# A decoder layer on one NeuronCore: order of transposes and units at the FFN entry, and the waits of the down steps

## What is computed

```python
x = x + rms_norm(mix @ w_o[l], attn_post_g[l])
h = rms_norm(x, ffn_pre_g[l])
y = conv_glu_ffn(h, w_gate[l], w_up[l], conv_w[l], conv_b[l], w_down[l])
x = x + rms_norm(y, ffn_post_g[l])

def conv_glu_ffn(h, w_gate, w_up, conv_w, conv_b, w_down):
    g = h @ w_gate                       # (256, 8192)
    u = h @ w_up
    ...                                  # g = causal conv over 3 tokens + conv_b
    return (gelu(g) * u) @ w_down
```

## Time and profile before

| | us |
|---|---|
| Time, median of 3 runs (1455.94 to 1456.43) | 1456.36 |
| The profiled execution | 1457.93 |
| Its span in the trace | 1454.9 |
| TensorE products busy | 1442.3 (99%) |
| VectorE busy | 1096.9 (75%) |
| ScalarE busy | 690.4 (47%) |
| GpSimd busy | 131.2 (9%) |

### The profile page before, as it was taken

One profiled execution on the slowest core, in us unless ns is written; L12 is line 12 of the kernel. 1 busy time (PEld: TensorE's weight loads), 2 busy tenths in 40 slices (PEclk: granted clock), 3 DMA queues, 4 the chain that ended last, 5 costly groups with the idle time before them and its releaser, 6 DMA issues.

```text
span 1454.9 us, 20961 instructions
## 1 busy us (share of the span) xinstructions
PE 1442.3 (99%) x6786; PEld 1208.1 (83%) x6786; DVE 1096.9 (75%) x1725; ACT 690.4 (47%) x855; POOL 131.2 (9%) x128
## 2 busy tenths in 40 slices
PE   9999999999999999999999999999999999999997
PEld 9888888888878888888888888888888888888886
DVE  6768686965688998888998888998888555555455
ACT  6445444554465444444444444444454444444443
POOL 0716160710000000000000000000000000000000
PEclk9999999999999999999999999999999999999999
DMA  7755565555566666666666666666665656666653
GB/s 257 221 185 164 175 199 174 170 164 181 167 209 197 191 195 191 189 200 189 195 194 189 191 197 190 199 189 192 193 192 178 206 192 191 196 190 193 195 189 128
DMA packets 141459, 276.24 MB, mean 190 GB/s; under 512 B 9040, under 2 KB 39024, under 8 KB 141168
## 3 DMA queue, kind: packets, MB, share of 16 engines
q1 hardware_dynamic: 140608, 274.71, 62.6%
q10 hardware_dynamic: 816, 1.09, 0.2%
HBM read 273.67 MB, written 2.10 MB: 190 GB/s over the span
## 4 chain that ended last, share of the span: by engine, by line
PE 96%; DVE 2%; DMA 1%; issue 1%; ACT 0%; DVEq 0%; ACTq 0%; POOL 0%; POOLq 0%
PE psum L1585 22%; PE psum L1381 20%; PE psum L1385 20%; PE psum L1383 20%; PE psum L1348 7%; PE psum L1352 4%; DMA stage<-in_w_qkv 1%; PE psum L1426 0%; DVE up_T L1117 0%; PE psum L1266 0%; PE psum L1432 0%; DVE y_out L1252 0%; DVE w_lo L802 0%; PE psum L1366 0%; PE psum L1425 0%
## 5 line engine op out<-in xcount | busy, mean ns | idle before, releaser
L466 ACT CAST w_hi<-stage 128x1024 fp32r<-128x1024 f32 x509 | 535.1, 1052 | 724.1 <-PE psum L1385 453.5
L802 DVE TENSOR_TENSOR w_lo<-stage,w_hi 128x1024 fp32r<-128x1024 f32 x509 | 633.4, 1245 | 309.9 <-ACT w_hi L466 298.6
L1381 PE MATMUL psum<-w_hi,hT 128*128 128x512 f32 x1144 | 446.4, 390 | 0.0
L1385 PE MATMUL psum<-w_hi,hT 128*128 128x512 f32 x1144 | 445.2, 389 | 0.0
L1383 PE MATMUL psum<-w_lo,hT 128*128 128x512 f32 x1144 | 445.1, 389 | 0.0
L1585 PE MATMUL psum<-w_hi,hT 128*128 128x512 f32 x1024 | 275.4, 389 | 0.7 <-DVE w_lo L802 0.7
L1385 PEld LDWEIGHTS psum<-w_hi,hT 128*128 128x128 f32 x1144 | 214.7, 188 | 44.8
L1381 PEld LDWEIGHTS psum<-w_hi,hT 128*128 128x128 f32 x1144 | 214.7, 188 | 44.5 <-DVE hT L831 0.3
L1383 PEld LDWEIGHTS psum<-w_lo,hT 128*128 128x128 f32 x1144 | 214.8, 188 | 44.2
L1585 PEld LDWEIGHTS psum<-w_hi,hT 128*128 128x128 f32 x1024 | 192.1, 188 | 40.9 <-DVE w_lo L802 1.1
L1585 PE MATMUL psum<-w_lo,hT 128*128 128x512 f32 x512 | 159.0, 389 | 0.0
(11 more groups left out here) (141 smaller groups left out, 855.1 us busy)
## 6 DMA issues: line engine op xcount, KB each, us to landing
stage<-in_w_gate SPq DMA_DIRECT2D x128, 512.0 KB, 3.7
stage<-in_w_up SPq DMA_DIRECT2D x128, 512.0 KB, 3.7
stage<-in_w_down SPq DMA_DIRECT2D x128, 512.0 KB, 4.1
stage<-in_w_qkv SPq DMA_DIRECT2D x93, 512.0 KB, 3.7
stage<-in_w_o SPq DMA_DIRECT2D x32, 512.0 KB, 4.0
stage<-in_w_qkv SPq DMA_DIRECT2D x6, 256.0 KB, 4.9
resid<-in_x SPq DMA_DIRECT2D x3, 512.0 KB, 9.2
post_g<-in_attn_post_g SPq DMA_DIRECT2D x1, 1024.0 KB, 6.7
```

Source lines behind the costliest of these rows:

```text
L466: nc.scalar.copy(w_hi[s][:, :], stage[s][:, :]).then_inc(s_hi, 1)
L802: nc.vector.tensor_tensor(w_lo[s][:, :], stage[s][:, :], w_hi[s][:, :].bitcast(F32), ALU.subtract).then_inc(s_lo, 1)
L1381: nc.tensor.matmul(o, lo[:, k, ts], w_hi[s][:, w], start=(k == 0), stop=False, skip_group_check=True)
L1385: ins = nc.tensor.matmul(o, hi[:, k, ts], w_hi[s][:, w], start=False, stop=last and kk == 1, skip_group_check=True)
```

## The change

It has these parts. On TensorE, the three products of ones behind the first tile's front units are taken out. The first transpose of tile 1 is issued inside the first tile's second front unit, behind its k tile 2; the other three follow that unit. The wait for `s_y_out` moves to the fourth transpose. The two front units of tile 1 follow each other. Then come T(2), the third gate unit in a form of its own (`third_unit`: by k tile, first the four products with the high part, then, behind a wait for that k tile's low part, the two with the low part), and T(3). In `ffn(0)` the loop starts at n = 3 and issues T(n+1) behind unit n, for n = 3 to 6. On VectorE, the fourth quarter update goes ahead of the first low part of tile 1. On ScalarE, the wait for all chunks between down step 0 and the loop is taken out, and each down step waits for its own chunk, `s_a_out` at i + 1, ahead of its first high part.

```diff
--- before.py
+++ after.py
@@ -693,8 +693,9 @@
                         kk = n // 4
                         wait_from(act, s_used, i * D_UNITS + (D_START + n - 4)
                                   if not (isinstance(i, int) and i == 0) else 0)
+                        if kk == 0:
+                            act.wait_ge(s_a_out, i + 1)
                         if isinstance(i, int) and i == 0:
-                            act.wait_ge(s_a_out, 1)
                             act.wait_ge(s_used, up_done(F_ITERS - 1) - CHUNK_UNITS + 2)
                         nc.scalar.copy(a_hi[kk][:, :, :],
                                        aT[:, bass.ds(i * 4 + 2 * kk, 2), :]).then_inc(s_a_hi, 1)
@@ -705,7 +706,6 @@
                     high_part(i * (D_UNITS // RING) + D_START // RING + n // RING, n % RING)
 
             down(0)
-            act.wait_ge(s_a_out, F_ITERS)
             with act.Fori(1, D_ITERS) as i:
                 down(i)
 
@@ -1103,8 +1103,8 @@
             add_y(0, 1, 0, P)
             add_y(0, 1, P, 2 * P)
             add_y(0, 1, 2 * P, 3 * P)
+            add_y(0, 1, 3 * P, 4 * P)
             front_row_low(1, 0)
-            add_y(0, 1, 3 * P, 4 * P)
 
             def transpose_blocks(rows, dst, first, count, signal):
 
@@ -1354,6 +1354,12 @@
                                                skip_group_check=True)
                 ins.then_inc(s_used, 1)
 
+            def second_rows(k):
+                pe.wait_ge(s_resid, 2 + k)
+                if k == FRONT - 1:
+                    pe.wait_ge(s_y_out, OUT_CHUNKS * TT)
+                front_transpose(1, k)
+
             def front_unit(n, t):
 
                 pe.wait_ge(s_lo, F_START + n + 1)
@@ -1366,8 +1372,27 @@
                         ins = nc.tensor.matmul(bank[GATE_BANK + t][:, :], a[:, k, ts], b[n][:, w],
                                                start=(k == 0 and a is hT_hi and b is w_hi), stop=False,
                                                skip_group_check=True)
+                    if t == 0 and k == FRONT - 2:
+                        second_rows(0)
                 if t == TT - 1:
                     ins.then_inc(s_used, 1)
+
+            def third_unit(n):
+
+                pe.wait_ge(s_lo, F_START + n + 1)
+                for kk in range(2):
+                    k = 2 * n + kk
+                    w = slice(kk * CHUNK, (kk + 1) * CHUNK)
+                    pe.wait_ge(s_hT_hi, KT - FRONT + k + 1)
+                    for t in range(TT):
+                        for b in (w_hi, w_lo):
+                            nc.tensor.matmul(bank[GATE_BANK + t][:, :], hT_hi[:, k, t * P:(t + 1) * P], b[n][:, w],
+                                             start=False, stop=False, skip_group_check=True)
+                    pe.wait_ge(s_hT_lo, KT - FRONT + k + 1)
+                    for t in range(TT):
+                        ins = nc.tensor.matmul(bank[GATE_BANK + t][:, :], hT_lo[:, k, t * P:(t + 1) * P],
+                                               w_hi[n][:, w], start=False, stop=False, skip_group_check=True)
+                ins.then_inc(s_used, 1)
 
             def row_unit(rnd, s, kp, banks, hi, lo, last, tiles=range(TT)):
 
@@ -1539,11 +1564,8 @@
 
             for n in range(FRONT // 2):
                 front_unit(n, 0)
-            pe.wait_ge(s_y_out, OUT_CHUNKS * TT)
-            stay_warm(3, ENTRY_BANKS[3])
-            for k in range(FRONT):
-                pe.wait_ge(s_resid, 2 + k)
-                front_transpose(1, k)
+            for k in range(1, FRONT):
+                second_rows(k)
 
             def transpose_updated(b):
                 pe.wait_ge(s_resid, resid_done(b // 2, 1))
@@ -1551,13 +1573,14 @@
 
             for n in range(FRONT // 2):
                 front_unit(n, 1)
-                pe.wait_ge(s_front_lo, TT * FRONT)
-                transpose_updated(n + 2)
+            transpose_updated(2)
+            third_unit(2)
+            transpose_updated(3)
 
             def ffn(i):
                 first = isinstance(i, int) and i == 0
                 for n in range(F_UNITS):
-                    if first and n < FRONT // 2:
+                    if first and n <= FRONT // 2:
                         continue
                     if first and n < KT // 2:
                         pe.wait_ge(s_hT_lo, KT - FRONT + 2 * n + 2)
@@ -1570,8 +1593,8 @@
                     kp = n % CHUNK_UNITS
                     row_unit(i * (F_UNITS // RING) + F_START // RING + n // RING, n % RING, kp,
                              (GATE_BANK, UP_BANK)[n // CHUNK_UNITS], hT_hi, hT_lo, kp == CHUNK_UNITS - 1)
-                    if first and n < 6:
-                        transpose_updated(n + 2)
+                    if first and n < 7:
+                        transpose_updated(n + 1)
 
             ffn(0)
             with pe.Fori(1, F_ITERS) as i:
```

## The result

The changed kernel takes 1469.04 us (median of 6 runs, 1467.87 to 1471.05) against 1455.78 us (6 runs) for the kernel before: ratio 1.0093, 95% interval 1.0083 to 1.0104, 13.3 us slower. The forecast was 1463.9 with a range of 1462.0 to 1467.5: the sign was right, the time lies 5.1 us above the forecast and above the range, and the step from the kernel before is 13.3 us where the sum had 7.5 (it started from 1456.36, the median of the first three runs). The profiled execution took 1468.49 us, span 1466.7 us.

A forecast was written before the change was run, and what follows sets the result against it. The tensor engine, 96% of the chain, was taken as the bound. Five exposed handoffs with the entry gain (+8.5 us) less 0.95 at the down steps gave +7.5 on 1456.36, so 1463.9 us, range 1462 to 1467.5.

The forecast's parts named there:

- the sum: Whole kernel: +8.5 us at the FFN entry and its handoffs less 0.95 at the down steps, +7.5 us, giving 1463.9.
- the rule weighed against the rows: Clock at the FFN entry: idleness brings half rate, but no row shows stalls this long recurring; the change could come out slower.
- The stretch from 24 to 27: Profile rows: tensor engine idle for 1.2 of 3 us, yet the granted clock stayed at 1.00.
- A: The forecast itself: five exposed handoffs at the full clock, 1463.9 us, range 1462.4 to 1465.2; chance 0.80.
- B: Exposed handoffs with a falling clock: 2.72 us more per cold unit, 1466.6 to 1477.5, two cold 1469.3; chance 0.12.
- part 3: Behind the third unit: units 3 to 7 each wait a 2.44 us handoff; +8.5 us, entry gain included.
- parts 1 and 2: FFN entry: early transpose, no ones, four updates in a row, third unit by k tile; 2.0 us won, bounds 0 and 2.4.
- Rival C: FFN entry: other work hides the conversions, so the handoffs' 10.5 us fall away and the gains stay, 1453.4; chance 0.04.
- part 4: Down projection start: ScalarE's earlier high part removes step 1's wait; gain 0.95 us, bounds 0.4 and 1.0.

The follow-up runs named there:

- order alone: Kernel before with one edit: T3 behind unit 2 and T(n+1) behind unit n, all else as it was, ones included; 1474.53 us, ratio 1.0122.

## Why the prediction was wrong

**The step that failed** is the one under the rule weighed against the rows, and the chance that follows from it: A (full clock) at 0.80, B (the clock falls) at 0.12. It rested on two rows. The stretch from 24 to 27 held a single stall, which says nothing of stalls in a row. The fall at the end of the kernel came some 2.4 us after the last product, and "my stalls of 2.1 us are just short" of it took that delay for a safe limit. The runs show in its place: units behind five stalls of 1.84 us, as the timeline counts them, ran at a mixed clock of 0.61 to 0.67 in eight of ten cases (changed kernel and order alone), while every stall ended at 1.00. That stalls bring the fall is shown by filling and by shortening them; what picks the unit is not. Rival B is what happened. That its number for two cold units (1469.3) met the median is luck, for its price was mis-sized: a unit was never cold from end to end, and cost 1.26 to 1.6 us, not 2.72, and three or more fell, not two.

**The handoffs** (part 3) were right: 2.44 us five times, unit periods of 5.30 us (407.16 to 412.46), T3 to unit 8 as worked out but for the clock. At the full clock the seam lost 8.8 us where the sum had 8.5; the order alone, in the kernel before, was enough for the loss, and putting T one unit ahead showed all else together to be a gain.

**The entry** (parts 1 and 2): T2 came 6.44 us behind the first product (394.16 to 400.60), forecast 6.33; T3 at 10.56, forecast 10.33. The gain before T3 was 1.8 us, not 2.0, within its bounds. Rival C's sum, 2.95 us under before if no handoff is exposed, was too good: with the transposes ahead the seam wins 0.92 us and the down step 0.97, 1.9 in sum, and the medians lie 1.9 apart. The waits of 0.64 us in front of T4 and of 0.4 behind it are as much as the 1.1 us that are missing.

**The down steps** (part 4): 0.97 us by the trace, 0.95 forecast; VectorE's loop entry shows no gap.

**The sum**: 8.8 (handoffs less entry gain) - 1.0 (down steps) + 4.6 (clock, profiled execution) = 12.4 us; the median run is 0.55 over the profiled one, which makes 12.95 of the 13.3 measured. Of the remaining 0.3 us, 0.2 is the first product of unit 8, behind the seam's end; the rest lies within the spread of the runs. The changed kernel's slowest runs, twice 1471.05 at a mean clock of 0.993 where the profiled one has 0.995, fit one or two more slow units; that is worked out from the clock alone.

## What to carry to other kernels

When transposes or conversions of a block are moved behind the unit ahead of them, write down what runs between a block's first step and its first use: if nothing does, the full handoff is paid for every block, and a gain at the entry is dwarfed by it. Cost a *repeated* stall with the clock in mind even where each is short, read the clock on the work behind the stall, and shorten the stall first: 1.18 us less in each of five stalls, 5.9 in sum, gave back 11.8. Products of ones ahead of a wait are not free if what is waited for hangs on the next instruction of the same engine.

## What the runs showed of the hardware

In the profiled executions TensorE's clock fell from 1.00 to 0.50 within the work behind nine of thirteen stalls of 1.84 us, each ahead of a unit of twelve products, and behind none of the stalls of 0.66, 0.95 or 1.40 us. The same order gave three slow units of five in one kernel and five of five in the other, and the same instructions up to unit 4 gave a slow unit 4 in one run and a fast one in another. While the clock is low, a product of 512 columns starts every 0.43 us against 0.23; a handoff whose transposes began at the low level took 2.79 and 2.70 us against 2.44. Products of ones that fill half of such a stall kept the clock up, which was worth 5.8 us here.
